# A hybrid decoder block on one Trainium2 core: mixer weights split once and reloaded, products and key steps reordered

## The reference, cut to what matters

```
u = rmsnorm(x, ln1_g); a_q, a_f, a_i, a_g, b_q, b_k, b_v = split(u @ w_in)
# A: 4 heads, gated linear recurrence in chunks of 64 tokens
forget = lb + (1 - lb) * sigmoid(a_f); key = 1 - forget; b = cumsum(log(forget))
a = tril((silu(a_q) * exp(b)) @ (key * exp(-b)).T)
o = a @ a_i + (silu(a_q) * exp(b)) @ S_before          # then rmsnorm, gain, silu(a_g)
# B: 8 heads of 64, window 128, ALiBi and sinks: softmax(scores) @ values, rmsnorm
h = x + concat(y_a, y_b) @ w_out
h = h + (silu(u2 @ w_gate) * (u2 @ w_up)) @ w_down     # u2 = rmsnorm(h, ln2_g)
out = rmsnorm(h, final_g)
```

## Time and profile before

| | |
|---|---|
| median of 3 runs | 2192.23 us (2192.19 to 2192.44) |
| profiled execution | 2193.37 us, of it the span 2191.7 us |
| PE busy | 2163.5 us, 99% |
| DVE, ACT, POOL busy | 1427.1, 975.8, 470.8 us |
| granted TensorE clock, mean | 0.998 |
| four superblocks of mixers | 24 to 914.5 us |
| first FFN and down | 914.5 to 1554 us |
| second FFN and down | 1554 to 2191 us |

### The profile page before, as it was taken

One profiled execution on the slowest core, in us unless ns is written; L12 is line 12 of the kernel. 1 busy time (PEld: TensorE's weight loads), 2 busy tenths in 40 slices (PEclk: granted clock), 3 DMA queues, 4 the chain that ended last, 5 costly groups with the idle time before them and its releaser, 6 DMA issues.

```text
span 2191.7 us, 29427 instructions
## 1 busy us (share of the span) xinstructions
PE 2163.5 (99%) x10836; PEld 1793.1 (82%) x10836; DVE 1427.1 (65%) x2136; ACT 975.8 (45%) x1782; POOL 470.8 (21%) x377
## 2 busy tenths in 40 slices
PE   8999999999999999999999999999999999999998
PEld 7887888888888888788888888888888888888886
DVE  5776678657865786857467675568665656555556
ACT  5443554445444554543433333346533333333445
POOL 2332034202320232132233330000233322220000
PEclk9999999999999999999999999999999999999999
DMA  4232332343235324543446566887432323327666
GB/s 130 89 120 68 125 97 87 117 144 102 82 102 159 106 59 131 196 144 123 128 164 218 199 235 204 260 269 259 163 121 92 120 92 117 100 91 241 225 207 225
DMA packets 262110, 323.86 MB, mean 148 GB/s; under 512 B 16464, under 2 KB 168016, under 8 KB 261968
## 3 DMA queue, kind: packets, MB, share of 16 engines
q1 hardware_dynamic: 261968, 321.98, 44.6%
HBM read 244.85 MB, written 77.07 MB: 147 GB/s over the span
## 4 chain that ended last, share of the span: by engine, by line
PE 82%; issue 9%; DVE 4%; POOL 3%; ACT 1%; DMA 1%; SPq 0%; DVEq 0%; POOLq 0%; ACTq 0%
PE M L1204 10%; PE M L1202 10%; PE M L1203 10%; PE M L904 5%; PE M L906 5%; PE M L905 5%; PE M L1227 3%; PE M L1229 3%; PE M L1228 3%; PE X L1227 3%; PE X L1229 3%; PE X L1228 3%; PE X L1204 3%; PE X L1202 3%; PE X L1203 3%
## 5 line engine op out<-in xcount | busy, mean ns | idle before, releaser
L2200 DVE TENSOR_TENSOR ring_lo<-ring_raw,ring_hi 128x1024 fp32r<-128x1024 f32 x154 | 189.6, 1232 | 161.8 <-ACT ring_hi L1633 161.6
L904 PE MATMUL M<-uhi,whi 128*128 128x512 f32 (+1 forms) x720 | 284.6, 395 | 2.9 <-DVE ulo L1769 2.9
L1747 DVE TENSOR_TENSOR wlo<-raw,whi 128x1024 fp32r<-128x1024 f32 x120 | 162.2, 1352 | 192.4 <-ACT whi L1282 192.0
L906 PE MATMUL M<-uhi,wlo 128*128 128x512 f32 (+1 forms) x720 | 277.7, 386 | 0.0
L905 PE MATMUL M<-ulo,whi 128*128 128x512 f32 (+1 forms) x720 | 277.3, 385 | 0.0
L1633 ACT ACTIVATE ring_hi<-ring_raw 128x1024 fp32r<-128x1024 f32 x154 | 163.3, 1060 | 228.1 <-DMA ring_raw<-a_scr 215.9
L1202 PE MATMUL M<-t_hi,wu_hi 128*128 128x512 f32 x616 | 240.6, 391 | 1.8 <-ACT snap L1589 1.8
L1204 PE MATMUL M<-t_hi,wu_lo 128*128 128x512 f32 x616 | 240.6, 391 | 0.0
L1203 PE MATMUL M<-t_lo,wu_hi 128*128 128x512 f32 x616 | 240.1, 390 | 0.0
L1282 ACT ACTIVATE whi<-raw 128x1024 fp32r<-128x1024 f32 x120 | 126.8, 1057 | 204.5 <-PE M L906 126.2
L2086 DVE TENSOR_TENSOR wu_lo<-fraw,wu_hi 128x512 fp32r<-128x512 f32 x132 | 125.3, 957 | 122.1 <-ACT wu_hi L1573 121.7
(11 more groups left out here) (283 smaller groups left out, 4967.5 us busy)
## 6 DMA issues: line engine op xcount, KB each, us to landing
raw<-in_w_in_dram SPq DMA_DIRECT2D x88, 512.0 KB, 3.9
ring_raw<-a_scr SPq DMA_DIRECT2D x154, 256.0 KB, 3.7
fraw<-in_w_gate_dram SPq DMA_DIRECT2D x44, 512.0 KB, 4.5
fraw<-in_w_up_dram SPq DMA_DIRECT2D x44, 512.0 KB, 4.8
a_scr<-au SPq DMA_DIRECT2D x88, 256.0 KB, 2.4
ring_raw<-t_scr SPq DMA_DIRECT2D x88, 256.0 KB, 3.0
ring_raw<-in_w_down_dram SPq DMA_DIRECT2D x66, 256.0 KB, 3.0
raw<-in_w_out_dram SPq DMA_DIRECT2D x32, 512.0 KB, 3.9
```

The lines of the kernel that those rows point to most:

```text
L904: mm(bank, whi[s][:, kb, :], hi, start=first, stop=False)
L906: return mm(bank, wlo[s][:, kb, :], hi, start=False, stop=last)
L1747: V.tensor_tensor(wlo[s][:, :, :], raw[s][:, :, :], whi[s][:, :, :].bitcast(F32), ALU.subtract).then_inc(s_lo[s], 1)
L2200: V.tensor_tensor(lo[:, :, :], raw_r[:, :, :], hi[:, :, :].bitcast(F32), ALU.subtract).then_inc(s_rowlo, 1)
```

## The change

In superblock 0 units are loaded and split as before, and SP also stores both parts of each (1 MB, `w_scr`). In superblocks 1 to 3 SP loads the split unit (1 MB) straight into one of three places; the third is the old raw buffer. ACT and DVE make no unit there. In superblock 0 `make_hi` waits for the store of the unit that held the place. On PE, pv(i - 1) and pv(i) are done together in every second slot, output comes before them, and update, iv_turn and keys after. POOL's 1 - forget moves one slot earlier, and the product with cuminv is done in two halves, each as its half of cuminv is there. The raw half of B22 now lies where h's first two blocks were, so its load waits for less and stands earlier on SP. Row 1 of `down` is split one product earlier. Semaphores for the gains are merged.

```diff
+        split = at("split", (P, 2, 2, KD, P), whi_at, F32R)
+        split_next = at("split_next", (P, 2, KD, P), raw_at, F32R)
+        wpair = [split[:, :, 0, :, :], split[:, :, 1, :, :], split_next[:, :, :, :]]
...
-            B22: pair_at("b22", h_at, h_at + 8 * K, operand),
+            B22: pair_at("b22", h_at + 8 * K, h_at, operand),
...
+        def place_of(it, n):
+            return n % 2 if it == 0 else (n + 2) % 3
...
+            def store_split(n):
+                s = n % 2
+                sp.wait_ge(s_lo[s], n // 2 + 1)
+                sp.dma_start(w_scr[n, :, :, :, :], wpair[s].bitcast(F32)).then_inc(s_wst[s], 16)
+
+            def load_split(it, n):
+                place = place_of(it, n)
+                if it == 1 and n == 0:
+                    for s in range(2):
+                        sp.wait_ge(s_lo[s], UH)
+                else:
+                    sp.wait_ge(s_group, it * UNITS + n - 2)
+                if it == 1:
+                    sp.wait_ge(s_wst[n % 2], 16 * (n // 2 + 1))
+                    if 0 < n < 3:
+                        sp.wait_ge(s_wst[place], 16 * UH)
+                sp.dma_start(wpair[place].bitcast(F32), w_scr[n, :, :, :, :]).then_inc(s_raw[place], 16)
...
                 if p == 0 and o == B22:
-                    sp.wait_ge(s_h, NSB * KD)
+                    sp.wait_ge(s_ftr, (NSB - 2) * 2 * TB + 4)
+                    sp.wait_ge(s_u, (NSB - 1) * TB)
...
+            def first_mixers():
+                for n in range(2, IN_GROUPS):
+                    if n > 2:
+                        load_in(n)
+                    store_split(n - 2)
...
+                load_split(1, 0)
+                store_split(UNITS - 2)
+                store_split(UNITS - 1)
+                load_split(1, 1)
...
+                    load_split(it, OUT_B + c)
+                    if last:
+                        load_operand(0, (B11, B21, T4, B22)[c])
...
-                    for begin, step in ((SCORE, scores), (P_TURN, p_turn), (PV, pv)):
+                    for begin, step in ((SCORE, scores), (P_TURN, p_turn)):
...
-                    for offset, step in ((KEYS, keys), (V_TURN, iv_turn), (UPDATE, update), (OUTPUT, output)):
+                    out_head = head_at(slot, OUTPUT)
+                    if out_head is not None:
+                        output_inside(it, out_head)
+                        output_before(it, out_head)
+                    i = step_at(slot, PV)
+                    if i is not None and i % 2:
+                        pv(it, i - 1)
+                        pv(it, i)
+                    for offset, step in ((UPDATE, update), (V_TURN, iv_turn), (KEYS, keys)):
...
+                if k:
+                    act.wait_ge(s_wst[s], 16 * k)
                 A(whi[s][:, :, :], raw[s][:, :, :], ACT.Copy).then_inc(s_hi[s], 1)
...
-                        if g == NG - 1 and o == A22:
+                        if g == NG - 1 and o == S4:
                             row_lo(p, 1)
...
-                pool.wait_ge(s_inv, 2 * n + 2)
-                G.tensor_tensor(key[:, :], key[:, :], cuminv[:, :], ALU.mult).then_inc(s_key, 1)
+                for part in range(2):
+                    half = slice(part * (T // 2), (part + 1) * (T // 2))
+                    pool.wait_ge(s_inv, 2 * n + 1 + part)
+                    G.tensor_tensor(key[:, half], key[:, half], cuminv[:, half], ALU.mult).then_inc(s_key, 1)
```

More of the change, by code:

```diff
@@ L883, in _ @@
             sp.dma_start(sinks[:, :], attn_sinks[0, :].partition_broadcast(P)).then_inc(s_par, 16)
-            load_in(0, 2)
-            for it in range(NSB):
+            load_in(2)
+            first_mixers()
+            for it in range(1, NSB):
                 mixers(it)
@@ L950, in group @@
                     wait_group_read(pe, it, slot - 3)
-                pe.wait_ge(s_lo[slot % 2], it * UH + slot // 2 + 1)
+                wait_unit_made(pe, it, slot)
                 if slot == 0:
@@ L954, in group @@
                 for k in range(KD):
-                    last = product(M[slot % 3][:, :], slot % 2, uhi[:, k, :], ulo[:, k, :], k,
+                    last = product(M[slot % 3][:, :], place_of(it, slot), uhi[:, k, :], ulo[:, k, :], k,
                                    k == 0, k == KD - 1)
@@ L984, in out_a @@
                         pe.wait_ge(s_oT, it * PAIRS + PAIRS)
-                    last = out_product(M[c][:, :], unit % 2, k, kk, c, first, last_k)
+                    last = out_product(M[c][:, :], place_of(it, unit), k, kk, c, first, last_k)
                 return last
@@ L1162, in out_b @@
                         for kk, k in enumerate(B_KS[c]):
-                            last = out_product(X[bank][:, :], n % 2, k, kk, b, k == 0, k == KD - 1)
+                            last = out_product(X[bank][:, :], place_of(it, n), k, kk, b, k == 0, k == KD - 1)
                         if c == 3 and b < TB - 1:
@@ L1427, in slots @@
                     n = unit_made_at(slot)
-                    if n is not None:
-                        wait_unit_used(act, it, n)
-                        make_hi(it, n)
+                    if it == 0 and n is not None:
+                        wait_unit_used(act, n)
+                        make_hi(n)
                     bank = M[slot % 3][:, :]
@@ L1547, in op_hi @@
                     wait_u_stored(act, NSB - 2)
+                if p == 0 and o == B22:
+                    act.wait_ge(s_h, NSB * KD)
                 A(OPERAND[o][0][:, :, :], OPERAND[o][2][:, :, :], ACT.Copy).then_inc(s_ophi, 1)
@@ L1910, in slots @@
                     n = unit_made_at(slot)
-                    if n is not None:
-                        wait_unit_used(dve, it, n)
-                        make_lo(it, n)
+                    if it == 0 and n is not None:
+                        wait_unit_used(dve, n)
+                        make_lo(n)
                     if mul is not None:
@@ L2027, in out_b @@
                 add(5)
-                unit(OUT_B + 5)
                 add(6)
```

197 lines of the change are left out of this document (105 added, 92 removed).

## The result

The changed kernel takes **2177.87 us** (median of five runs, 2177.09 to 2178.95), the kernel before 2192.44 (2192.19 to 2195.5): a ratio of 0.9926, with a 95% interval of 0.9913 to 0.994. It is faster, by 14.6 us. The prediction said 2167.8 us and 2164.8 to 2174.5, so 10.1 us of the expected gain are missing and the range does not hold the result.

The account below looks back on a forecast made before the run. PE, busy 99% of the span, was taken as the bound. Terms of -12.2 - 9.3 - 3.7 + 0.8 = -24.4 us took the profiled 2193.37 to 2169.0; with the median 1.1 lower, 2167.8 us, range 2164.8 to 2174.5.

Parts of the forecast that it names:

- Term 1: Mixers on PE: pairing pv saves the price per half-array run, 12.2 us in four superblocks (11 to 13).
- Rival 3: Mixers on PE: a run of 16 saves nothing over two of 8, giving 2180 us; chance 0.04.
- Term 2: Mixers: 13 of PE's waits for key, output and head_turn go, saving 9.3 us (5 to 10.5).
- Rival 2: Mixers: the waits move instead of going, term 2 brings 1 us, giving 2176 us; chance 0.08.
- Term 3: FFN start: B22's earlier load removes PE's pause and the slow clock behind it, saving 3.7 us (0 to 3.9).
- At nothing: Changes priced at 0: units taken off ACT and DVE beyond term 2, and 1 MB loads instead of 512 KB.
- Rival 1: FFN start: B22 brings nothing, landing late among other operands or ACT meeting another wait, giving 2171.5 us; chance 0.1.
- Term 4: Start of down, twice: row 1's wait moves to row 3 and becomes 1.1 us, costing 0.8 us (-1.4 to +1.6).
- the border's 3 us: Border of superblocks 0 and 1: loads and stores in line cost 0, or 3 us if each takes 7.7 us more.

Follow-up runs that it names:

- e7: Changed kernel with PE's step order, POOL's key, B22 and row 1 of down put back, so only splitting once is new: 2186.13 us, ratio 0.9970.
- e6: e5 with pv in every slot instead of two in every second slot, so the new order without pairs: 2188.95 us, ratio 0.9981.
- e5: Kernel before with only the change's new order of PE's steps, pairs of pv included: 2184.18 us, ratio 0.9962.
- e12: Changed kernel with POOL's key product back in one piece and its first step in the old slot: 2179.30 us, ratio 0.9934.
- e11: Kernel before with the change's new handling of operand B22 alone: 2193.65 us, ratio 0.9997.
- e8: e4 with operand T3's parts made ahead of the first gate weights' parts on ACT and DVE: 2173.75 us, ratio 0.9913.
- e10: e8 with POOL's sums for the second group of weights held until the first group's S4 part is made: 2171.48 us, ratio 0.9898.
- e9: e8 with operand B22's parts made one product later, behind the weight part of the sixth product: 2173.66 us, ratio 0.9904.
- e13: Changed kernel with only POOL's sums for the second group held until the first group's S4 part is made: 2178.30 us, ratio 0.9928.
- e1: Changed kernel with the first FFN gate weights asked for before operand B22: 2177.64 us, ratio 0.9929.
- e2: Changed kernel with the parts of row 1 of down made at product A22 again, as before: 2175.71 us, ratio 0.9920.
- e3: e1 with B22 handled as in the kernel before, SP waiting for the last sum of h before loading it: 2177.48 us, ratio 0.9927.
- e4: Changed kernel with the edits of both e1 and e2: 2174.55 us, ratio 0.9914.

## Why the prediction was wrong, and where it was right

**Term 1 held.** 12.2 us forecast; beside the freed DVE (e7 against the changed kernel) the order is worth 11.7, of it 11.1 outside the gaps, a pair's run lasts 1.07 for the 1.03 forecast, 32 half-array runs are gone, and e6 shows that the pairs themselves matter (0.31 us for a run, where the step had 0.36). Rival 3, which the prediction drew from the Trainium skill (TensorE: Matmul & The Clock Gate, The mechanism), a weight load overlapping with products in flight only in another row group, is refuted: the run of 16 takes 1.07 us where two runs of 8 take 1.20, and without pairs (e6) the mixers end 4.2 us later. The same section of the Trainium skill also lets a load into the background weight buffer go ahead, which the prediction left out. One thing was left unsaid: on its own, in e5, the order brings 8.3 us. The term holds in full only beside term 2.

**Term 2 held in size, with a wrong division.** 9.3 forecast; 9.0 come with e7's splitting and 0.5 more in superblock 0's gaps. But the working built the key's part from the half product (0.6) and the transposes (0.4), with DVE as an addition. e7 and e12 show the reverse: DVE's freed 1.22 us per slot remove every one of these waits of superblocks 1 to 3 alone, the halves none. The two steps were alternatives, not a sum. Rival 2 did not come; e5 is what it would have looked like.

**Term 3 failed: "I take back 1.83 + 0.16 + 1.7 = 3.7 us".** The step followed one chain, SP to ACT to the restart of PE behind its fourth product, and asked what removes its wait. It did not ask what is late next on DVE. e11 answers on the kernel before: the parts of the sixth product, behind b_lo beside POOL, 2.0 us. Nor did it ask what else the earlier load sets off: the up weights land 7.5 us earlier, POOL starts on them 6.0 us earlier, and it is POOL that makes b_lo late. The bound "0 (the clock pause comes from another wait)" had no room for a loss, and the measured value was +1.3.

**"At nothing" failed for the end of superblock 3.** "At 391 GB/s PE kept its pace" is true of the units, and says nothing of the loads whose landing is wanted next. The gate weights were asked for 10.7 us before the end of the mixers and landed in up to 9.6 where they had taken 3.8, and ACT and DVE could no longer prepare the first products in advance. Unit 22 took 10.5 us where the working had 7.7, and landed just when it was wanted. Splitting alone (e7) already brings the loss at the FFN start to 5.68, most of it at a gap of 3.3 us where the kernel before waits 2.2 for B22, with the slow clock in both; the order alone (e5) has 2.07. Rival 1 had the right place and both its reasons (late among the operands, another wait), but priced them as a gain not made (2171.5), not as a loss beyond it. That rival's sum with a loss of 1.3 instead would have been 2172.8, inside the range. It is terms 3 and 4 together that leave it.

**Term 4: the mechanism was right, the size was off.** "So the wait moves to row 3 and becomes 1.1: plus 0.4 each." It did move to row 3, by the au store and SP as said. The wait there is shorter, 0.59 above a normal distance, but rows 4 and 5 are late by the same chain (0.43 and 0.49): SP asks for them behind row 3, and ACT and DVE get them one after the other. Three rows instead of one: 1.5 us for the first pass and 1.8 for the second, against 0.6 each at row 1 in the kernel before. That is 2.1 of the 2.7 us; the other 0.6 stand at later rows. Undoing it is worth 1.6 and 2.9 us in the two ledgers, 1.3 and 3.1 in time. The bound of +1.6 was short.

**The baseline.** The forecast took 1.1 us off because the profiled execution stood above the median of three runs. With more runs the kernel before has medians of 2192.4 to 2194.4, so a difference of 1.1 between an execution and its median was no property of the kernel.

The range left out what a loss of two places at once would give. Its upper end, 2174.5, was rivals 1 and 2 with the border's 3 us; a sum with term 3 at +1.3 and term 4 at +2.7 gives 2167.8 + 5.0 + 1.9 = 2174.7 before the small rests.

## What to carry to other kernels

When a wait is removed at the end of a chain, list for each engine what it has to make for the next two or three steps of the bottleneck, with its durations beside its neighbours, and find the second latest. Ask also which engine the edit lets start earlier, and beside what it will then run: here a removed wait of 1.8 us was followed by one of 2.0, which POOL's earlier start had made. When loads double, look for the stretch where the DMA is already full, and price there not the units that are pipelined but the first load of the next phase, by its landing in the line. And two edits that each would remove the same wait (a key in halves, a freed DVE) must not both be counted.

## What the hardware showed that I had not expected

**DVE and POOL block each other for whole instructions.** b_lo (128x2048) takes 2.29 us when it starts first and 3.37 when POOL is already in a sum; wl_lo and wu_lo (128x512) take 0.68 and up to 1.8; POOL's sums take 1.30 with nothing in their way and up to 3.3 or 3.4 behind such a DVE instruction. The differences, 1.1 on DVE and 2.0 to 2.1 on POOL, are the rest of the other's instruction. The Trainium skill (SBUF — State Buffer, SBUF: two separate sides) calls the port pair that the two share an exclusive lock: who starts first has it for the whole instruction, and the other is blocked. The trace of e8 agrees, to 0.2 us in each of three steps, and e10 shows the price, 2.2 us of PE's time from a POOL that had nothing urgent to do.

**The clock behind a gap.** In the profiled executions PE's starts went to the half level (0.427 us apart) for 6 to 8 products behind a gap of 2.2 to 3.3 us in the kernel before, e7, e8, e9, e12 and e13, and stayed at full level behind gaps of 2.3 to 2.45 us in the changed kernel, e1, e2, e3, e4 and e11. It costs about 1.5 us when it comes, and the length of the gap alone does not tell whether it does. The prediction had counted 1.7 us of it as a gain of B22's load. With one profile of each kernel it stays open whether a kernel has it in every execution; e13's missing gain in the ledger is one such case.
